# Even page order across turns, half copies of the query, memory tokens through the weight ring

## The reference

```python
h = rmsnorm(x, g_mix)
z = h @ w_in                       # fox q, k, v, forget gate; gla q, k, v, r, gate
o_f = fox_sample(q, k_new, v_new, logf, k_past, v_past, logf_past)   # 8 requests, 2048 cached tokens each
o_f = fox_prompt(q, k, v, logf)    # 8 heads, 256 tokens
S, o_g = gla_chunk(S, q, k, v, log_alpha)                            # 4 heads
x = x + concat(o_f, rmsnorm(o_g, g_head) * silu(r)) @ w_out
m = rmsnorm(mem_prompt, g_mem); mk, mv = m @ w_xk, m @ w_xv          # 256 memory tokens
x = x + cross_attn(rmsnorm(x, g_cross), mk, mv, w_xq, w_xo)
x = x + swiglu(rmsnorm(x, g_ffn), w_gate, w_up, w_down)
y = rmsnorm(x, g_final)
```

## Time and profile before

| | us |
|---|---|
| three runs | 1702.38, 1702.67, 1703.0 |
| the profiled execution | 1704.66 |
| its span, first to last instruction | 1702.9 |
| PE busy | 1560.3 (92%) |
| DVE busy | 1048.8 (62%) |
| ACT busy | 619.2 (36%) |
| POOL busy | 229.7 (13%) |

### The profile page before, as it was taken

The page is one execution under the profiler, slowest core; times in us unless marked ns, Lnnn a source line. Parts: engine busy times, 40 slices in busy tenths (PEclk is TensorE's granted clock), DMA queues, the critical chain, the costliest instruction groups (busy, mean ns, idle before and its releaser), DMA issues.

```text
span 1702.9 us, 32739 instructions
## 1 busy us (share of the span) xinstructions
PE 1560.3 (92%) x12269; PEld 1436.2 (84%) x12269; DVE 1048.8 (62%) x3212; ACT 619.2 (36%) x722; POOL 229.7 (13%) x331
## 2 busy tenths in 40 slices
PE   5989989878789899999679999999999999999997
PEld 4979766656677668999368999999999999999996
DVE  5469788978778777565635555554444555554444
ACT  4333232221224354444445334333333334333443
POOL 3001212212222122231111000000000000000221
PEclk9999989889899889999789999999999999999998
DMA  8458999989799898744413545544555555553553
GB/s 319 147 180 296 391 333 401 328 320 353 259 392 360 298 341 325 303 175 162 130 55 128 191 175 176 192 174 136 177 179 200 187 181 174 189 178 128 185 182 123
DMA packets 85411, 388.48 MB, mean 228 GB/s; under 512 B 9128, under 2 KB 18096, under 8 KB 63552
## 3 DMA queue, kind: packets, MB, share of 16 engines
q1 hardware_dynamic: 35712, 230.96, 38.2%
q0 software_dynamic: 39376, 143.15, 22.5%
q10 hardware_dynamic: 10224, 13.12, 2.2%
HBM read 377.10 MB, written 10.10 MB: 227 GB/s over the span
## 4 chain that ended last, share of the span: by engine, by line
PE 73%; DVE 16%; DMA 5%; ACT 4%; issue 2%; DVEq 0%; POOLq 0%; ACTq 0%; SPq 0%; POOL 0%
PE bank L1486 21%; PE bank L1487 21%; PE bank L1488 21%; DVE page L1038 5%; DMA page<-vc_dram 4%; DVE wlo L975 4%; PE bank L1618 2%; ACT whi L578 1%; DVE wlo L941 1%; PE bank L1567 1%; ACT whi L541 1%; PE bank L1641 1%; DVE rstd L967 1%; PE bank L1783 1%; DVE g_d L1145 0%
## 5 line engine op out<-in xcount | busy, mean ns | idle before, releaser
L1486 PE MATMUL bank<-hh,whi 128*128 128x264 f32 (+1 forms) x2368 | 697.5, 295 | 24.6 <-DVE wlo L975 20.7
L1487 PE MATMUL bank<-hl,whi 128*128 128x264 f32 (+1 forms) x2368 | 679.1, 287 | 0.0
L1488 PE MATMUL bank<-hh,wlo 128*128 128x264 f32 (+1 forms) x2368 | 678.7, 287 | 0.0
L941 DVE TENSOR_TENSOR wlo<-raw,whi 128x2048 fp32r<-128x2048 f32 (+1 forms) x174 | 356.2, 2047 | 281.3 <-ACT whi L541 281.3
L541 ACT ACTIVATE whi<-raw 128x2048 fp32r<-128x2048 f32 (+1 forms) x174 | 299.3, 1720 | 543.0 <-PE bank L1488 543.0
L1486 PEld LDWEIGHTS bank<-hh,whi 128*128 128x128 f32 x2368 | 454.7, 192 | 49.7 <-issue 25.0
L1487 PEld LDWEIGHTS bank<-hl,whi 128*128 128x128 f32 x2368 | 455.2, 192 | 3.4 <-issue 3.1
L1488 PEld LDWEIGHTS bank<-hh,wlo 128*128 128x128 f32 x2368 | 452.9, 191 | 0.0
L1038 DVE CUSTOM_DVE_ANT_0 page<-page,qb 128x128 f32<-128x128 f32 x1024 | 226.3, 284 | 27.3 <-DMA page<-kc_dram 15.0
L1486 PE MATMUL bank<-f_hi,whi 128*128 128x264 f32 x704 | 201.9, 287 | 7.5 <-DVE f_lo L1458 7.5
L1488 PE MATMUL bank<-f_hi,wlo 128*128 128x264 f32 x704 | 201.3, 286 | 0.0
(11 more groups left out here) (283 smaller groups left out, 1524.5 us busy)
## 6 DMA issues: line engine op xcount, KB each, us to landing
raw<-p_gu_dram SPq DMA_DIRECT2D x88, 1024.0 KB, 4.8
page<-kc_dram POOLq DMA_DIRECT2D x128, 512.0 KB, 8.1
page<-vc_dram POOLq DMA_DIRECT2D x128, 512.0 KB, 7.9
raw<-p_in_dram SPq DMA_DIRECT2D x48, 1024.0 KB, 7.9
raw<-p_dn_dram SPq DMA_DIRECT2D x64, 704.0 KB, 4.1
raw<-p_out_dram SPq DMA_DIRECT2D x16, 1024.0 KB, 5.0
raw<-p_mem_dram SPq DMA_DIRECT2D x8, 1024.0 KB, 8.0
x_res<-x_fm_dram SPq DMA_DIRECT2D x8, 528.0 KB, 9.9
```

Of the source, the lines that this page charges most:

```text
L941: tt(wlo[:, k % 4, 0:blocks * P], raw[:, k % 4, 0:blocks * P], whi[:, k % 2, 0:blocks * P], ALU.subtract).then_inc(S("w_split"), 1)
L1486: mm(out, blk(whi, k % 2, b), rh, start=start, stop=False)
L1487: mm(out, blk(whi, k % 2, b), rl, start=False, stop=False)
L1488: return mm(out, blk(wlo, k, b), rh, start=False, stop=stop)
```

## The change

It does this:

- `QUARTERS`: quarters of panels per turn go from 32, 32, 12, 12, 20, 20, 24, 16, 24 (turns 0 to 8) to 28, 36, 12, 12, 24, 24, 24, 16, 16. Turns 7 and 8 have one in every part.
- `values`: turn t has one value page in each part, request t - 2's last five in parts 0 to 4 and request t - 1's first eleven in parts 5 to 15. Turn 8 has two pages a part in parts 5 to 12. `prob` is double, 8 columns wide instead of 32, and the bank of the outputs is cleared once instead of `prob`.
- `q_copy` waits for each half by itself: the first half for the fourth head of key page 15 (`q_half`), the second for the whole page.
- The narrow projection and the small work behind it go from the prologue to part 1 of turn 0 and behind. The rest of turn 0's gate work moves back by two parts.
- The norm's sum: POOL adds the squares of groups 0 and 1, and of 2 and 3, so that PE sums 8 blocks instead of 16, four behind panel 0 and four behind the second quarter of panel 1.
- Memory tokens go as two 1 MB loads into places 0 and 1 of `raw`, behind panels 44 and 45. The panels from 48 on stand two places further round the ring (`ring`). Panel 49's load waits until panel 47 is multiplied, those of 50 and 51 until the tokens in their place are used. The tokens' high and low parts are made in parts 0 to 3 of turn 7, four blocks a part, where panel 48 is multiplied too.
- The GLA decay differences are made as two half subtractions each, with the right sign, so that ACT's pass for the absolute value (line 671) is gone.
- `take_o`, `extract` and `take_heads` move from parts 0 and 1 to parts 5 to 8; `HEAD_AT`, the state loads and the silu move by some parts.

Core of the diff (of the two `memory_turn`, ScalarE's stands first, then VectorE's; both now come ahead of the part's other work):

```diff
-QUARTERS = ([2] * 16,) * 2 + ([1, 1, 1, 0] * 4,) * 2 + ([1, 1, 1, 2] * 4,) * 2 + (
-    [2, 1] * 8, [2] * 4 + [0] * 6 + [1, 1, 1, 1, 2, 2], [2, 1] * 8)
-VALUES = ([0] * 4 + [1, 1, 2] * 4,) * 8 + ([0] * 4 + [2] * 8 + [0] * 4,)
-HEAD_AT = (1, 3, 7, 9, 13, 18, 19, 24)
+QUARTERS = ([2, 2, 2, 1] * 4, [2, 2, 2, 3] * 4) + ([1, 1, 1, 0] * 4,) * 2 + ([2, 1] * 8,) * 3 + ([1] * 16,) * 2
+HEAD_AT = (0, 2, 6, 8, 12, 17, 23, 24)
...
 def values(t, j):
-    first = sum(VALUES[t][:j])
-    return range(first, first + VALUES[t][j])
+    if j < 5:
+        return [(t - 2, 11 + j)] if t >= 2 else []
+    if t == 8:
+        return [(7, v) for v in (2 * j - 10, 2 * j - 9) if v < 16]
+    return [(t - 1, j - 5)] if t >= 1 else []
...
+def ring(p):
+    return p if p < IN else p + 2
...
             def memory(g):
-                sp.dma_start(mraw[:, 4 * g:4 * g + 4, :], mem_fm[:, 4 * g:4 * g + 4, :]).then_inc(S(f"group_in{g}"), 16)
+                sp.wait_ge(S("mm_done"), IN + g - 3)
+                sp.dma_start(raw[:, g, :], mem_fm[:, g, :]).then_inc(S(f"w_in{g}"), 16)
...
             def weights(p):
                 name, n = ("in", p) if p < IN else ("mem", p - IN)
-                if p >= 4:
-                    sp.wait_ge(S("mm_done"), p - 3)
-                sp.dma_start(raw[:, p % 4, :], io["p_" + name][P * n:P * n + P, :]).then_inc(S(f"w_in{p % 4}"), 16)
+                if 2 <= n < 4 and p >= IN:
+                    sp.wait_ge(S("n_lo_done"), C + 8 * n - 8)
+                    sp.wait_ge(S("n_sq"), 2 * n - 2)
+                elif p >= 4:
+                    sp.wait_ge(S("mm_done"), p - 1 if IN <= p < IN + 2 else p - 3)
+                sp.dma_start(raw[:, ring(p) % 4, :], io["p_" + name][P * n:P * n + P, :]).then_inc(S(f"w_in{ring(p) % 4}"), 16)
...
+            xch = Chain(pool, "pool_chain0")
             for g in range(4):
                 pool.wait_ge(S(f"group_in{g}"), 16)
                 xs = x_res[:, 4 * g:4 * g + 4, :]
-                pool.tensor_tensor(x_sqs[:, 4 * g:4 * g + 4, :], xs, xs, ALU.mult).then_inc(S("n_sq"), 1)
+                ins = pool.tensor_tensor(x_sqs[:, 4 * g:4 * g + 4, :], xs, xs, ALU.mult)
+                if g % 2:
+                    xch.link(ins)
+                    pool.tensor_tensor(x_sqs[:, 4 * g - 4:4 * g, :], x_sqs[:, 4 * g - 4:4 * g, :], x_sqs[:, 4 * g:4 * g + 4, :], ALU.add
+                                       ).then_inc(S("x_acc"), 1)
...
             def q_copy(t):
                 act.wait_ge(S("q_ps"), t + 1)
-                if t:
-                    act.wait_ge(S("k_used"), 16 * t)
                 for n in range(2):
-                    ins = act.activation(qb[:, 512 * n:512 * n + 512], bank[2 + n][:, :], ACT.Copy)
-                ins.then_inc(S("q_b"), 1)
+                    if t:
+                        act.wait_ge(S(("q_half", "k_used")[n]), (t, 16 * t)[n])
+                    act.activation(qb[:, 512 * n:512 * n + 512], bank[2 + n][:, :], ACT.Copy).then_inc(S("q_b"), 1)
...
             def memory_turn(j):
-                if 8 <= j < 12:
-                    g = j - 8
-                    act.wait_ge(S(f"group_in{g}"), 32)
+                if j < 4:
+                    if j % 2 == 0:
+                        act.wait_ge(S(f"w_in{j // 2}"), 16 * (IN // 4 + 1))
+                    for c in range(4 * j, 4 * j + 4):
+                        norm_hi(1, c, 2, hh, mem_raw(c), MEM)
+                if 1 <= j < 5:
+                    if j > 1:
+                        act.wait_ge(S("n_ss"), 4 + j - 1)
+                    act.activation(m_sq, mem_four(j - 1), ACT.Square).then_inc(S("n_sq"), 1)
...
             def memory_turn(j):
-                if 9 <= j < 13:
-                    g = j - 9
-                    for c in range(4 * g, 4 * g + 4):
-                        norm_lo(1, c, 2, mraw[:, c, 0:MEM], hh, hl, MEM)
+                if j < 4:
+                    for c in range(4 * j, 4 * j + 4):
+                        norm_lo(1, c, 2, mem_raw(c), hh, hl, MEM)
+                elif j == 7:
+                    norm_scale(1, MEM)
+                    panel_evac(IN)
...
             def gla_turn(i, j):
                 if j == 3:
                     act.wait_ge(S("g_diff"), i + 1)
-                    act.activation(g_d[:, 0:LEVELS, :], g_d[:, 0:LEVELS, :], ACT.Abs).then_inc(S("g_abs"), 1)
                     act.activation(g_eb, g_b, ACT.Exp)
-                    act.activation(g_d[:, LEVELS, :], g_d[:, LEVELS, :], ACT.Exp)
-                    act.wait_ge(S("g_abs"), i + 1)
-                    act.activation(g_d[:, 0:LEVELS, :], g_d[:, 0:LEVELS, :], ACT.Exp, scale=-1.0).then_inc(S("g_exp"), 1)
+                    act.activation(g_d, g_d, ACT.Exp).then_inc(S("g_exp"), 1)
```

More of the change, by code:

```diff
@@ L84, in page_places @@
                 where["k", t, j] = len(where)
-            for v in values(t, j) if t else ():
-                where["v", t - 1, v] = len(where)
+            for u, v in values(t, j):
+                where["v", u, v] = len(where)
     for kind in ("xk", "xv"):
@@ L392, in _ @@
             first_x(3)
-            for p in range(2, IN + 3):
+            for p in range(2, IN):
                 weights(p)
-            sp.wait_ge(S("mm_done"), IN)
-            for g in range(4):
-                memory(g)
-            for p in range(IN + 3, IN + 8):
+            memory(0)
+            memory(1)
+            for p in range(IN, IN + 8):
                 weights(p)
@@ L450, in _ @@
                         fetch("k", t, j)
-                    for v in values(t, j) if t else ():
-                        fetch("v", t - 1, v)
+                    for u, v in values(t, j):
+                        fetch("v", u, v)
             for b in range(8):
@@ L472, in build, with mem_raw @@
         HN_BANKS = (2, 3, 6, 7)
+        def mem_raw(c):
+            return raw[:, c // 8, MEM * (c % 8):MEM * (c % 8) + MEM]
         def a_set(n):
@@ L1000, in _ @@
             norm_scale(0, T)
-            dve.memset(prob, 0.0)
             dve.wait_ge(S("nw_hi"), 1)
@@ L1498, in panel @@
                         pe.wait_ge(S("n_lo_done"), C * NORMED[name] + b + 1)
-                    last = three(bank[k % 2][:, 0:n], k, b, hh[:, b, 0:n], hl[:, b, 0:n], b == 0, b == blocks - 1)
+                    last = three(bank[k % 2][:, 0:n], (k + 2) % 4, b, hh[:, b, 0:n], hl[:, b, 0:n], b == 0, b == blocks - 1)
                 last.then_inc(S("mm_done"), 1)
@@ L1510, in quarter @@
                         pe.wait_ge(S("n_lo_done"), (0 if p == 0 else C) + b + 1)
-                    last = three(bank[p % 2][:, 0:n], p % 4, b, hh[:, b, 0:n], hl[:, b, 0:n], b == 0, b == C - 1)
+                    last = three(bank[p % 2][:, 0:n], ring(p) % 4, b, hh[:, b, 0:n], hl[:, b, 0:n], b == 0, b == C - 1)
                 if q == 3:
@@ L1522, in out_panel @@
                     hi, lo = (b, 8 + b) if b < 8 else (16 + b, 24 + b)
[L1523 removed]
+                    last = three(bank[c % 2][:, 0:T], (c + 2) % 4, b, zr[:, hi, :], zr[:, lo, :], n == 0, n == C - 1)
                 last.then_inc(S("mm_done"), 1)
@@ L1905, in first_columns @@
         out += [splits[0] + P * h, splits[1] + P * h]
-    return out + [gr + P * h for h in range(8)]
+    return out + [gr + P * h for h in (4, 5, 6, 7, 0, 1, 2, 3)]
 def kernel(**x):
```

222 lines of the change are left out of this document (114 added, 108 removed).

## The result

The changed kernel takes 1692.7 us (median of 10 runs, 1688.0 to 1696.9), the kernel before beside it 1704.1 (10 runs). The ratio is 0.9932, with a 95% interval of 0.9913 to 0.9952: 11.5 us faster, where 27.6 were forecast. The profiled execution has a span of 1693.5 us.

The account below looks back on a forecast made before the run. No one engine bounds the whole: PE sets turns 1, 6 and 8, DVE 2 and 3, mutual waits 4 and 5. Terms through turn 8 sum to -27.6 us, giving a median of 1675.0; own range 1667 to 1683, wide range 1663 to 1696.

Parts of the forecast that it names:

- The forecast for turns 4 and 5: Turns 4 and 5, with one more panel each, come to 65.0 and 64.5 us: -4.7 and -4.4.
- The panel on top of the old time: Rival, turns 4 and 5: hand-offs tie the parts, the sixth panel costs 5.8 less 4.0; 1688 us, chance 0.17.
- the pages' pace of 320 to 325 GB/s: Rival, turns 4 and 5: transfers stay at their old rate, turns take 73 and 72 us; 1691 us, chance 0.12.
- The part of the sum at the borders that was given to the half copy: Turn borders: copying the query's first half alone (0.6 us) helps shorten DVE's wait for the query.
- that rival: Turn borders: query halves gain nothing, as ACT waits for PE's spread; +3.8 us, 1679, inside the forecast, no own chance.
- Panel 49's load now waits for the end of panel 47: Turn 7: 12 us from panel 47's end, PE stands 8.9 us; with the panel-free stretch gone, the turn changes by -3.8.
- The sign that it named: Start of turn 7: one PE wait of 8 to 9 us, released by a low part behind a cast awaiting a load.
- if turn 7 grows: Turn 7: sign that the forecast is wrong; the turn was forecast at 69 us, from 72.8.
- Prologue: Before turn 0: narrow projection -5.8, split sum -0.6, cleared `prob` -0.5, POOL's additions holding DVE +2.8; sum -4.1 us.
- The bound without the additions: Prologue: without the cost of POOL's additions it would gain 6.9 us.
- Nothing changes but places in the ring: Behind turn 8: no change in time, 0 us.
- The clock rival: Rival, turns 7 and 8: thin work keeps PE's clock at 0.68, +41.5 us, 1716 us, slower than before; chance 0.10.

Follow-up runs that it names:

- experiment 4: Changed kernel with only panel 48's cast and split moved late, behind the heads' work of part 15 of turn 6; 0.9908 of the kernel before, 1688.7 us.
- experiment 1: Changed kernel with casts and splits of both panels 48 and 49 moved behind the heads' work; 0.9893 of the kernel before, 1686.8 us.
- the second profile: The changed kernel run and profiled once more, unchanged; 0.9953 of the kernel before, 1696.4 us.
- experiment 9: Changed kernel with late casts, squares only and late keys, plus PE's query spread early in turns 0, 1, 4, 5; 0.9786 of the kernel before, 1668.0 us.
- Experiment 8: Changed kernel with late casts, squares only and late keys, plus the tokens' high parts a part ahead of the squares; 0.9832 of the kernel before, 1676.9 us.
- experiment 2: Changed kernel without POOL's additions, PE summing 16 blocks behind panel 0 as before; 0.9879 of the kernel before, 1686.9 us.
- Experiment 3: Changed kernel with the cross attention's eight key pages fetched beside the output projection's additions; 0.9894 of the kernel before, 1687.3 us.
- experiments 1 and 5: The second of these: changed kernel with late casts, squares only and late keys together; 0.9863 of the kernel before, 1680.0 us.

## Why the prediction was right or wrong

**Turns 2 to 5: right in size, in part by luck.** -2.0, -2.0, -4.9 and -3.7 for -1.8, -2.0, -4.7 and -4.4. The forecast for turns 4 and 5 was 62 us of PE's work and 3 of idle time. PE was busy for 58.2 and 58.6 us and idle for 7.1 and 6.5: the sixth panel cost less than its 5.8, since the clock rose from 0.90 and 0.88 to 0.97, and PE stood longer than forecast. The two errors cancel. The panel on top of the old time (71.5 and 70.7) and the pages' pace of 320 to 325 GB/s are refuted by the windows. The part of the sum at the borders that was given to the half copy (0.6 a border) had the wrong reason: that rival held, and DVE still waits 2.1 to 5.0 us for the query at the borders to turns 3 to 6. It had such a wait at the first two of these in the kernel before (3.9 and 4.1, now 2.1 and 3.3), not at the borders to turns 5 and 6.

**Turns 6 and 7: the step that failed.** "Panel 49's load now waits for the end of panel 47" is true, and experiment 4 shows it at its forecast price. But the two token loads move panel 48's load too, from the end of panel 44 to the end of panel 46, one panel ahead of its use, and its cast stands at the head of ACT in part 13. The prediction counted one load of two. The sign that it named, one wait of PE of 8 to 9 us released by a low part, shows in experiment 4 (8.7); the 8.4 us in the kernel after are near it by chance, being a wait for the softmax behind the other load. The 14.4 us are made up so, but for rounding: 5.6 are the stand between panels 47 and 48 (17.6 us for the 12 worked out), and experiment 1 shows that both loads' waits together are worth 10 us. 5.0 lie ahead of it in turn 6, which takes 69.2 us to the end of panel 47 where 67.3 less the 3.1 behind it, 64.2, were forecast. Of these, 3.1 are the clock (0.95; the second profile has 66.1 at 1.00), and some 2 are the late spread of the query, which experiment 9 takes away. 3.6 lie in turn 7 behind the start of panel 48, 63.7 for 60.1. There 3 us of waits were allowed for, and PE is idle for 6.9, of which the low parts of the tokens make 1.5 and 3.3. Experiment 8 takes part of it away. The prediction's sign for this failure, "if turn 7 grows", looked at the wrong turn: turn 7 fell from 73.1 to 63.7 us, and turn 6 grew, from 67.2 to 86.9.

**Prologue: the mechanism right, the size short.** POOL's additions do hold DVE: the last low part ends at 29.3 us, forecast 29.2, though in another order than forecast (each of the first four low parts beside one operation of POOL, and not one low part behind three operations in a row). The Trainium skill's page SBUF — State Buffer, section SBUF: two separate sides, says that the operation that starts first keeps the port pair to its end; the alternating 2.2 us low parts and POOL operations agree with it. What was mis-sized is PE behind it. The forecast let PE end panel 0 0.6 us behind the last low part, at 29.8; it ended at 31.9, since its matmuls came every 0.22 us and not every 0.12 until 31.4. That is 2.1 us. The trace of the kernel before had shown it: its last low part ends at 24.8 us and PE ends panel 0 2.0 behind it, with the same 0.22 us up to 23.9. Panel 2 then starts 2.3 us later than forecast (45.8, not 43.5), and takes 7.2 us behind a stand of 4.3 at a granted clock of 0.79 from 42 to 50 us, where the kernel before needs 5.9 at 1.00: 1.3 more (in the six other profiles with the additions it took 8.3 to 8.7). The two make the 3.6, and 3.4 of it are a low clock that the sum had put at nothing. The bound without the additions, -6.9, is borne out: experiment 2 gives -5.8, the five other profiles without them -6.0 to -8.5.

**Behind turn 8: a cost put at nothing.** "Nothing changes but places in the ring" overlooked that a shorter turn 8 pushes transfers together. The last key page of the cross attention is now issued 4 us ahead of the end of turn 8 (671.7 for 675.8), in the kernel before 8 us ahead (680.0 for 688.3), and the input blocks and the fourth output panel's load come right behind it. Experiment 3 shows 2.5 us of the 3.1; the cross attention, 89.0 us for 88.5, is the rest.

**Turn 8 and turns 0 and 1.** -8.4 for -7.5, at a transfer share of 1.00: the pages did press, less than 1.1 us. Turns 0 and 1 gained 1.4 where +1 stood; PE's idle time shrank in turn 1 from 4.2 us to 1.4, and in turn 0 from 5.9 to 4.9, 3.8 us for the 2 forecast, and the clock of turn 1 rose from 0.97 to 1.00. For turn 8, that the pages cost less than 1.1 us is inferred from the sum.

**The clock rival** did not hold where it was placed: 0.97 and 1.00 in turns 7 and 8. But the clock is there in other stretches that the sum took at full speed: 2.1 and 1.3 us in the prologue, 3.1 in turn 6, 0.62 in the stand of the kernel after. It also makes two profiles of kernels with the same waits differ by 3 us a turn (turn 7 in experiments 1 and 5).

In all, 16 of the 27.6 us never came. The result lies in the wide range (1663 to 1696) and outside the forecast's own (1667 to 1683), and the terms that failed had left out a wait on a load or a hand-off that is only just in time, and the low clock behind such stands.

## What to carry to other kernels

When transfers are put into a ring of places, list every load behind them with the event that now releases it and the event that first needs it; each one that lost its lead has a price, and the price is that of all that is queued behind its cast or its wait, which moving the waiting instruction behind the ready ones takes away at little cost (10 us gained, 1.2 given back). A finer hand-off (a copy in halves) is worth nothing while the producer ahead of it comes last; here it was the place of the producer's work, the spread, that counted. When two profiles differ by a few us, compare PE's idle time and its clock apart, before a wait is blamed. And ask of a queue that runs dry earlier what it issues next, and what that shares the transfers with.
